# Reordering the beginning of a diffusion trunk: group products between modulation pieces, and two gate pieces moved into the first feed-forward tiles

## What is computed

```python
mod = silu(cond) @ w_mod[0] + b_mod[0]          # six vectors: shift, scale, gate, twice
h   = rms_norm(x, g) * (1 + scale0) + shift0
p   = window means of h minus h, for windows 2, 4, 8, 16, each on its own 256 channels
y   = einsum('blgc,gcd->blgd', p, pool_w) * pool_scale
x   = x + gate0 * rms_norm(y, g)
h   = rms_norm(x, g) * (1 + scale1) + shift1    # input of the feed-forward block
```

## Time and profile before

| | before |
|---|---|
| timed, median of 3 (least, most) | 2003.72 us (2002.95, 2004.3) |
| profiled execution, its own time | 2000.1 us |
| span of the trace | 1998.4 us |
| busy: TensorE, VectorE, ScalarE, GpSimd | 96%, 59%, 46%, 35% |
| mean granted clock of TensorE | 0.984 of full speed |
| transfers | 322.74 MB, mean 162 GB/s |

### The profile page before, as it was taken

One profiled execution on the slowest core, in us unless ns is written; L12 is line 12 of the kernel. 1 busy time (PEld: TensorE's weight loads), 2 busy tenths in 40 slices (PEclk: granted clock), 3 DMA queues, 4 the chain that ended last, 5 costly groups with the idle time before them and its releaser, 6 DMA issues.

```text
span 1998.4 us, 29996 instructions
## 1 busy us (share of the span) xinstructions
PE 1926.6 (96%) x11750; PEld 1708.8 (86%) x11750; DVE 1178.4 (59%) x1793; ACT 928.0 (46%) x1575; POOL 698.9 (35%) x507
## 2 busy tenths in 40 slices
PE   6899999999999989999999999999999979999998
PEld 4789998899996767999987957999987967899986
DVE  3657751666536685777615844777714684777722
ACT  3544442544547645444425325544425444644422
POOL 0233334232345553332343732322342521323342
PEclk8999999999999989999999998999999989999999
DMA  9874456443331147544365655643375513433442
GB/s 398 339 262 127 136 200 231 150 127 119 115 99 38 38 149 307 198 127 125 134 233 183 206 152 211 231 127 120 102 254 179 180 38 116 137 119 125 127 127 74
DMA packets 80139, 322.74 MB, mean 162 GB/s; under 512 B 8976, under 2 KB 17664, under 8 KB 66688
## 3 DMA queue, kind: packets, MB, share of 16 engines
q1 hardware_dynamic: 78496, 318.93, 46.3%
q10 hardware_dynamic: 1504, 1.91, 0.3%
HBM read 315.70 MB, written 5.10 MB: 161 GB/s over the span
## 4 chain that ended last, share of the span: by engine, by line
PE 87%; DVE 4%; DMA 3%; ACT 2%; issue 2%; POOL 1%; SPq 0%; DVEq 0%; POOLq 0%; ACTq 0%
PE pair L1900 18%; PE pair L1902 18%; PE pair L1901 18%; PE pair L1932 8%; PE pair L1933 8%; PE pair L1934 8%; PE pair L1869 2%; PE pair L2053 2%; PE pair L2147 1%; DMA mod_raw<-in_w_mod 1%; DMA raw<-in_ffn_in 1%; PE pair L2278 1%; PE pair L2058 1%; PE pair L2067 1%; PE pair L2252 1%
## 5 line engine op out<-in xcount | busy, mean ns | idle before, releaser
L796 POOL TENSOR_TENSOR w_lo<-raw,w_hi 128x512 fp32r<-128x512 f32 (+1 forms) x375 | 589.8, 1575 | 1052.0 <-ACT w_hi L930 1051.9
L1900 PE MATMUL pair<-h_hi,w_hi 128*128 128x386 f32 (+1 forms) x2008 | 686.6, 342 | 2.1 <-DVE h_lo L1430 2.1
L1902 PE MATMUL pair<-h_hi,w_lo 128*128 128x386 f32 (+1 forms) x2008 | 681.4, 339 | 0.0
L1901 PE MATMUL pair<-h_lo,w_hi 128*128 128x386 f32 (+1 forms) x2008 | 680.7, 339 | 0.0
L1324 DVE TENSOR_TENSOR w_lo<-raw,w_hi 128x512 fp32r<-128x512 f32 x339 | 405.9, 1200 | 330.1 <-ACT w_hi L930 329.8
L930 ACT ACTIVATE w_hi<-raw 128x1024 fp32r<-128x1024 f32 x375 | 392.5, 1051 | 287.9 <-PE pair L1934 227.9
L1900 PEld LDWEIGHTS pair<-h_hi,w_hi 128*128 128x128 f32 (+1 forms) x2008 | 379.0, 189 | 10.9 <-issue 9.6
L1901 PEld LDWEIGHTS pair<-h_lo,w_hi 128*128 128x128 f32 (+1 forms) x2008 | 379.8, 189 | 0.9
L1902 PEld LDWEIGHTS pair<-h_hi,w_lo 128*128 128x128 f32 (+1 forms) x2008 | 379.1, 189 | 0.3
L1489 DVE SCALAR_TENSOR_TENSOR acc<-pair,taps,acc 128x385 f32<-128x385 f32 x176 | 108.8, 618 | 197.4 <-ACT acc L1044 197.3
L1044 ACT ACTIVATE acc<-pair,taps 128x386 f32<-128x386 f32 x176 | 117.3, 666 | 211.7 <-PE pair L1902 211.6
(11 more groups left out here) (304 smaller groups left out, 2109.3 us busy)
## 6 DMA issues: line engine op xcount, KB each, us to landing
raw<-in_ffn_in SPq DMA_DIRECT2D x176, 512.0 KB, 3.5
raw<-in_ffn_out SPq DMA_DIRECT2D x88, 512.0 KB, 3.6
mod_raw<-in_w_mod SPq DMA_DIRECT2D x36, 1024.0 KB, 6.7
mod_base<-in_w_mod SPq DMA_DIRECT2D x31, 1024.0 KB, 7.0
mod_more<-in_w_mod SPq DMA_DIRECT2D x18, 1024.0 KB, 21.5
raw<-in_ssd_conv SPq DMA_DIRECT2D x32, 512.0 KB, 3.5
raw<-in_ssd_z SPq DMA_DIRECT2D x16, 512.0 KB, 3.5
raw<-in_ssd_out SPq DMA_DIRECT2D x16, 512.0 KB, 3.6
```

What stands on the lines that cost most here:

```text
L796: pool.tensor_tensor(w_lo[:, m % SLOTS, 0:w], raw[:, m % SLOTS, 0:w], w_hi[:, m % SLOTS, 0:w].bitcast(F32), ALU.subtract).then_inc(w_low_p ...
L1900: ten.matmul(to, wh, h_hi[:, k, cols], start=k == 0, stop=False, skip_group_check=True)
L1901: ten.matmul(to, wh, h_lo[:, k, cols], start=False, stop=False, skip_group_check=True)
L1902: ins = ten.matmul(to, wl, h_hi[:, k, cols], start=False, stop=k == KD - 1, skip_group_check=True)
```

## The change

Five edits, all in layer 0:

1. The output product of the pool runs per group. A group's product for the blocks starts when its own two channel tiles are ready, and pieces 8 to 11 stand between the groups. The banks of the pool tiles and of vector 1 change so that this is free of conflicts. The two chunks of `pool_w` are rounded one after tile 4 and one after tile 6 of the pool loop instead of both ahead of tile 4, and their low halves stand in VectorE's loop likewise.
2. ScalarE's and VectorE's part of `transition0` is re-ordered; ScalarE's rounding of the first feed-forward chunks goes behind the last sum of squares, and VectorE makes the third `unit_stage` ahead of the second `unit_low`.
3. On TensorE, pieces 12 to 15 go ahead of the first `turn_unit`, 16 and 17 behind the second, 18 and 19 behind the third.
4. Only two of gate1's four pieces run ahead of tile 0; the other two stand behind tiles j = 2 and 3, and the eight pieces of layer 1 behind j = 4 to 11. SyncE's loads are shifted to fit.
5. Gate1 is read by VectorE behind tile 3, and turned behind tile 5 in place of 3.

The hunks are in the order of the file: constants and SyncE, then ScalarE, VectorE and TensorE.

```diff
+GATE1_BEFORE = 2
+GATE1_TURNED_BEHIND = 5
...
-            i = j - INSIDE_FIRST + MOD_PIECES
-            return end_pieces(0)[i] if l == 0 and MOD_PIECES <= i < len(end_pieces(0)) else None
+            i = j - INSIDE_FIRST + GATE1_BEFORE
+            return end_pieces(0)[i] if l == 0 and GATE1_BEFORE <= i < len(end_pieces(0)) else None
...
-                            load_to(s.n0 + INSIDE_FIRST + i + 2)
+                            load_to(s.n0 + INSIDE_FIRST + MOD_PIECES - GATE1_BEFORE + i + 2)
...
             def transition0(n):
                 gate_copy(0)
                 first(0, 0)
+                first(0, 1)
                 gate_copy(1)
-                first(0, 1)
                 second(0, 0)
+                first(0, 2)
                 second(0, 1)
-                first(0, 2)
+                second(0, 2)
                 round_to(n + 2)
-                second(0, 2)
...
-                    if k == POOL_DEPTH:
-                        round_to(2)
+                    if k in (POOL_DEPTH, POOL_DEPTH + 2):
+                        round_to(k // 2 - 1)
...
                 coefficient(0, 1)
                 before_weigh(0, 0)
+                before_weigh(0, 1)
                 weigh(0, 0)
-                before_weigh(0, 1)
                 residual(0, 0)
+                before_weigh(0, 2)
                 weigh(0, 1)
                 residual(0, 1)
                 unit(0, 0)
-                before_weigh(0, 2)
+                weigh(0, 2)
+                residual(0, 2)
                 unit(0, 1)
                 mod_vector(3)
                 coefficient(0, 2)
-                weigh(0, 2)
-                residual(0, 2)
+                unit(0, 2)
                 mod_vector(4)
-                unit(0, 2)
                 unit_stage(0, 0)
                 unit_stage(0, 1)
                 unit_low(0, 0)
+                unit_stage(0, 2)
                 unit_low(0, 1)
-                unit_stage(0, 2)
                 low_to(n + 1)
...
-                mod_vector(phases[1][0])
-                coefficient(0, 3)
...
-                if k == KD:
-                    low_to(2)
+                if k in (POOL_DEPTH + 1, POOL_DEPTH + 3):
+                    low_to(k // 2 - 1)
...
+                v2 = 2 * MOD_PIECES
+                ten.wait_ge(sums_copied, len(WINDOWS))
+                for g in range(2):
+                    mod_piece(v2 + g)
+                    for c in range(3):
+                        ins = product(g, c)
+                ins.then_inc(w_used, 1)
+                mod_piece(v2 + 2)
+                ten.wait_ge(pooled_scaled, KD)
+                for c in range(2):
+                    product(2, c)
+                mod_piece(v2 + 3)
+                for c in range(2):
+                    product(3, c).then_inc(out_done, 1)
+                ten.wait_ge(coef_ready, 2)
+                spread_gate(0)
+                ten.wait_ge(mod_read, 3)
+                product(2, 2)
+                product(3, 2).then_inc(w_used, 1)
+                ten.wait_ge(gate_copied, 1)
+                spread_gate(1)
+                for p in range(3 * MOD_PIECES, 4 * MOD_PIECES):
+                    mod_piece(p)
                 ten.wait_ge(gate_copied, 2)
                 turn_unit(0, 0)
                 ten.wait_ge(pre_ready, 2)
                 turn_unit(0, 1)
+                for p in range(4 * MOD_PIECES, 4 * MOD_PIECES + 2):
+                    mod_piece(p)
                 ten.wait_ge(pre_ready, 3)
                 turn_unit(0, 2)
+                for p in range(4 * MOD_PIECES + 2, START_VECTORS * MOD_PIECES):
+                    mod_piece(p)
                 ten.wait_ge(stage_act, 1)
                 ten.wait_ge(stage_dve, 1)
-                fill(0, 0, MOD_PIECES)
+                fill(0, 0, GATE1_BEFORE)
```

More of the change, by code:

```diff
@@ L342, in pooled_bank @@
         def pooled_bank(k):
-            return bank((6, 7, 0, 1)[k % POOL_DEPTH])
+            return bank((6, 7, 1, 3)[k % POOL_DEPTH])
         def tile_bank(j):
@@ L516, in squares @@
             if t == 0:
-                return 3 + ((0, 2), (1, 3), (4, 5))[c][which]
+                return 3 + ((0, 2), (1, 4), (3, 5))[c][which]
             return 3 + (2 * event(t, c) + which if t < 2 * DEPTH - 1 else 2 * event(t, 0) + c)
@@ L1045, in ffn_in @@
                                    bias=taps[:, l, j, 3:4]).then_inc(acc_ready, 1)
-                    if j == 3:
+                    if j == gate_turned_behind(l):
                         copy_row(2 * l)
@@ L1498, in ffn_in @@
                     low_to(s.n0 + j + 5)
+                    if l == 0 and j == 3:
+                        mod_vector(phases[1][0])
+                        coefficient(0, 3)
                     if l == 0 and j == 7:
@@ L1860, in mod_piece @@
                 ten.wait_ge(mod_loaded[mod_slot[p]], 16 * mod_uses[p])
-                if j == 0 and i == 2:
-                    ten.wait_ge(mod_read, 1)
+                if j == 0 and i in (1, 2):
+                    ten.wait_ge(mod_read, i)
                 if j == 0 and i in (3, 4):
@@ L2325, in pool_mix @@
                 for k in range(KD):
-                    if k in (2, 3):
-                        ten.wait_ge(sums_copied, k - 1)
+                    if k == 2:
+                        ten.wait_ge(sums_copied, 2)
                     if k >= POOL_DEPTH:
@@ L2333, in pool_mix @@
                             mod_piece(p)
-                for p in range(2 * MOD_PIECES, 3 * MOD_PIECES):
-                    mod_piece(p)
-                chunk_ready(0)
-                chunk_ready(1)
-                ten.wait_ge(pooled_lo, KD)
-                for c in range(3):
-                    cols = slice(AT[c], AT[c] + P)
-                    if c == 1:
-                        ten.wait_ge(mod_read, 2)
-                    if c == 2:
-                        ten.wait_ge(mod_read, 3)
-                        ten.wait_ge(sums_copied, len(WINDOWS))
-                    for g in range(4):
-                        to = pair[c][:, g * 256:(g + 1) * 256]
-                        for kk in range(2):
-                            k, at = 2 * g + kk, (2 * (g % 2) + kk) * 256
-                            wh, wl = (v[:, g // 2, at:at + 256] for v in (w_hi, w_lo))
-                            ten.matmul(to, h_hi[:, k, cols], wh, start=kk == 0, stop=False, skip_group_check=True)
-                            ten.matmul(to, h_lo[:, k, cols], wh, start=False, stop=False, skip_group_check=True)
-                            ins = ten.matmul(to, h_hi[:, k, cols], wl, start=False, stop=kk == 1, skip_group_check=True)
-                        if c == 2 and g % 2:
-                            ins.then_inc(w_used, 1)
-                    if c < 2:
-                        ins.then_inc(out_done, 1)
-                        if c == 0:
-                            ten.wait_ge(coef_ready, 2)
-                            ten.wait_ge(pooled_scaled, KD)
-                        else:
-                            ten.wait_ge(gate_copied, 1)
-                        spread_gate(c)
@@ L2364, in pool_mix, with product @@
-                for p in range(3 * MOD_PIECES, 4 * MOD_PIECES - 1):
+                def product(g, c):
+                    chunk_ready(g // 2)
+                    ten.wait_ge(pooled_lo, 2 * g + 2)
+                    cols, to = slice(AT[c], AT[c] + P), pair[c][:, g * 256:(g + 1) * 256]
+                    for kk in range(2):
+                        k, at = 2 * g + kk, (2 * (g % 2) + kk) * 256
+                        wh, wl = (v[:, g // 2, at:at + 256] for v in (w_hi, w_lo))
+                        ten.matmul(to, h_hi[:, k, cols], wh, start=kk == 0, stop=False, skip_group_check=True)
+                        ten.matmul(to, h_lo[:, k, cols], wh, start=False, stop=False, skip_group_check=True)
+                        ins = ten.matmul(to, h_hi[:, k, cols], wl, start=False, stop=kk == 1, skip_group_check=True)
+                    return ins
@@ L2367, in pool_mix @@
                 turn_unit(0, 0)
-                for p in range(4 * MOD_PIECES - 1, START_VECTORS * MOD_PIECES):
-                    mod_piece(p)
                 ten.wait_ge(pre_ready, 2)
                 turn_unit(0, 1)
+                for p in range(4 * MOD_PIECES, 4 * MOD_PIECES + 2):
+                    mod_piece(p)
                 ten.wait_ge(pre_ready, 3)
                 turn_unit(0, 2)
+                for p in range(4 * MOD_PIECES + 2, START_VECTORS * MOD_PIECES):
+                    mod_piece(p)
                 ten.wait_ge(stage_act, 1)
                 ten.wait_ge(stage_dve, 1)
-                fill(0, 0, MOD_PIECES)
+                fill(0, 0, GATE1_BEFORE)
             ten.wait_ge(cond_ready, 1)
```

8 lines of the change are left out of this document (5 added, 3 removed).

## The result

| | before | after |
|---|---|---|
| timed, median (least, most) | 2003.51 us (1996.17, 2006.21), 20 runs | 2008.37 us (2003.62, 2013.62), 20 runs |
| ratio after to before | | 1.0031, 95% interval 1.0023 to 1.0038 |
| profiled execution, its own time | 2000.1 us | 2007.64 us |

The change makes the kernel slower by 0.31%: by the ratio 6.2 us (4.6 to 7.6), by the medians 4.9. The forecast was 5.4 us.

A forecast was written before the change was run, and what follows sets the result against it. The beginning was held by transfers and short chains, then by TensorE's own work from tile 0. Terms 0.9 - 0.8 + 2.4 + 1.1 + 1.8 = 5.4 us on 2003.72 gave 2009.1 us, 8-in-10 range 2003.2 to 2011.5.

The forecast's parts named there:

- both places at half clock: TensorE around the first two turns and at tile 0's start: half clock costs +1.1 and +1.8 us; chance 0.58.
- The step called decisive: TensorE's order puts shift1's last pieces behind the turns, ending at 70.3, so unit_stage waits for them: +0.9 us.
- The rival by which the clock holds: TensorE keeps full clock in one or both places; 2006.2 us if both, chance 0.28 including one.
- The chain that pays: Rival: VectorE's chain ends earlier, tile 0 starts near 75.6; gain at most 3.0 us, 2000.7; chance 0.09.
- First product 39.6, spread 49.6: TensorE's pool products start near 39.6 instead of 45.64; first gate spread follows at 49.6, against 48.53.
- Gate copy, weigh, VectorE's chain 10.6: After the spread: gate copy 2.0 us, weigh done at 53.8, VectorE then runs 10.6 us without waiting, to 64.4.
- `unit_stage` at 71.0, or 72 with the half clock: Start of unit_stage after shift1 is read, against 70.05 before: +0.9 us, later still at half clock.
- exactly the term: Half clock on the two pieces behind the second turn, 0.56 longer each: +1.1 us.
- Tail -0.8: From unit_stage to tile 0, the third unit_stage fills VectorE's idle time, winning 0.8 of 1.8 us.
- Two pieces +2.4: Two gate1 pieces moved from TensorE's wait to between feed-forward tiles cost 1.2 us each: +2.4 us.
- Half clock at tile 0 +1.8: After idling ahead of tile 0, TensorE runs its first about 4.1 us at half clock: +1.8 us.
- Tile 0 at 79.3 to 80.5: Sign expected in the changed profile: first feed-forward tile starts at 79.3 to 80.5, against 79.24 before.

The follow-up runs named there:

- a_turns: Changed kernel with TensorE's pieces 15 to 19 back in the order before the change, all ahead of the second turn; ratio to the kernel before 1.0009.
- b_pieces: Kernel before with only pieces 15 to 19 in the changed order, and shift1 read behind VectorE's third unit; ratio to the kernel before 1.0017.
- b_gate2: Kernel before with only the gate1 part: two pieces ahead of tile 0, two more between tiles, gate row turned later; ratio to the kernel before 1.0012.
- a_gate4: Changed kernel with all four gate1 pieces ahead of tile 0 again; ratio to the kernel before 1.0021.
- a_both: Changed kernel with pieces 15 to 19 ahead of the second turn and four gate1 pieces ahead of tile 0; ratio to the kernel before 1.0001.
- a_warm2: Changed kernel with unread matmuls added on idle TensorE: five before the first turn, four before the second, seven behind the second gate1 piece; ratio to before 1.0021.
- c_tail: c_ahead with VectorE's second unit_low ahead of the third unit_stage again, as before the change; ratio to the kernel before 0.9991.
- b_round: Kernel before with only ScalarE's rounding of the two feed-forward chunks moved behind its last sum of squares; ratio to the kernel before 1.0005.
- c_ahead: Changed kernel with pieces 15 to 19 all ahead of the first turn and four gate1 pieces ahead of tile 0; ratio to the kernel before 0.9989.
- c_early: c_ahead with the products of block 2 with groups 0 and 1 moved behind the first gate spread; ratio to the kernel before 0.9991.
- c_early3: c_early with three gate1 pieces ahead of tile 0 instead of four; ratio to the kernel before 0.9990.
- a_three: a_turns with three gate1 pieces ahead of tile 0 instead of two; ratio to the kernel before 1.0010.

## Why the prediction was right, and where its terms were off

The forecast was 5.4 us with both places at half clock, and the timed difference is 4.9 by the medians and 6.2 by the ratio. The step called decisive was: pieces 18 and 19 behind the third turn hold `unit_stage`. The chain of waits shows it in the trace, and a_turns and b_pieces show what the order of pieces 15 to 19 costs, the one by taking it away (0.22%), the other by doing it alone (0.17%). The second cost, two pieces moved out of a wait, is shown by b_gate2 (0.12%). With a_gate4's 0.10% and a_both's 0.01% for the rest, the parts add up to 0.28 to 0.35%, around the change's 0.31%; each part is known to about 0.1%. The rival by which the clock holds falls with the trace (0.50 through most of 62.8 to 69.6 and 76 to 86.6) and with a_warm2. The chain that pays came out nowhere: tile 0 would have had to start before 76.8.

Term by term, by the trace of after:

- *First product 39.6, spread 49.6.* Measured 39.81 and 50.57. The ten products took 7.8 us where I had 7.2 (0.78 each and not 0.72, the first one of a group being longer behind a piece), the pieces 1.0 each.
- *Gate copy, weigh, VectorE's chain 10.6.* Measured 1.99, 2.19 and 10.5 us. Right.
- *`unit_stage` at 71.0, or 72 with the half clock.* Measured 74.10. Of the 3.1 us over 71.0, 1.0 is the later spread, 1.1 the two pieces at half clock (2.98 for 1.9, exactly the term), 0.9 the second turn at half clock. I had left that turn out, and where I priced one I took 1.40 from the earlier trace rows, a turn that ran only in part at half clock: a whole one takes 1.94.
- *Tail -0.8.* Measured 0.0: 9.18 us from `unit_stage` to tile 0, before 9.19; c_tail confirms it. I saw that the step must wait for GpSimd, and still took half of the idle time as won. It waits 1.27 us, and the low half behind it takes 2.02 where it took 1.57.
- *Two pieces +2.4.* In the trace 97.75 to 98.75 and the longer matmul behind it, 1.2 each, as taken from the earlier trace rows. The other pieces between the tiles and the later gate row were put at nothing; one piece waited 0.5 us for its transfer.
- *Half clock at tile 0 +1.8.* Measured 1.5 (3.4 us at 0.32 for 0.18).
- *Tile 0 at 79.3 to 80.5.* Measured 83.28, outside what was named as a sign. The path was right and the terms on it were too small.

By the two traces the loss is larger than forecast: 8.6 us up to the marker, and 7.5 between the two profiled executions as a whole. The terms ahead of tile 0 were too small by 2.8 us (+1.2 said, +4.0 found); behind it 4.2 were said and 4.6 found, of which 0.5 is the wait for a transfer. That the timed 4.9 to 6.2 lies so near the 5.4 is therefore luck in part: the sum was too small for the pair of executions that were traced, and that pair lies further apart than the timed runs do. The execution traced before was 3.4 us faster than its median, the one after only 0.7.

The clock in the products does not explain that gap. Both traces have it full there. In the three other traces with the old order the four products ahead of the first spread took 1.3 to 2.4 us longer; in five of the eight traces with the ten products of the new order ahead of it these took 1.3 to 1.5 us longer. By these means the old order loses some 0.6 us more than the new one, an estimate from few traces. The new product order was never run alone, so what it gives back, and where the rest of the gap lies, stays open.

From the marker to the end it takes 1593.4 us (a_turns) to 1600.1 (b_round), whatever the edit. Why, stays open too, and it is why a single trace can't stand for the timed difference.

## What to carry to other kernels

A piece of filler work belongs ahead of the work that waits for its data, in the engine's idle time, not behind it: behind the last step of a chain it becomes the last step. Before such a piece is moved, ask who reads its result and where that reader then stands. And where an engine idles ahead of a long dense stretch, the work that fills that wait costs nothing and can keep TensorE's clock; moving it into the dense stretch costs its length and often, on top, the slow start. c_ahead is the version to take; its gain over the kernel before is 0.4 to 4.2 us by its interval, and c_early, c_early3 and c_tail can't be told from it.

## What the runs showed of the hardware

The half clock came back where TensorE had waited between short bursts, but not after every such wait and not always in the same place: the same four products ahead of the first spread ran at full clock in one trace and wholly or in part at half clock in three. At tile 0, idle times of 4.74, 5.71, 4.83 and 5.77 us (after, a_turns, a_three, b_gate2) led to half clock, and one of 2.33 to 2.51 us to full clock (a_gate4, b_pieces, a_warm2); but a_both, with 2.71, had half clock, b_round, with 4.05, kept the full clock for its first matmuls only, and c_tail entered half clock in its last gate piece without any longer wait than c_ahead, which kept its clock. With four gate pieces ahead, tile 0 began at full clock in four traces (before, a_gate4, b_pieces, c_ahead) and wholly or partly at half clock in four (a_both, b_round, c_early, c_tail); with two or three pieces and nothing else in the wait it began at half clock in all five. The Trainium skill (TensorE: Matmul & The Clock Gate, "HAM oscillation — how this bites in real kernels") describes the pattern, and its half of the cold time as the loss is close: 0.44 here.

VectorE and GpSimd hold each other up when both read two blocks at once, and which one pays depends on who is there first. With GpSimd idle a low half of 512 columns takes VectorE 0.64 us (1.28 for two, in c_tail at 77.38), and an undisturbed weight half takes GpSimd 1.25 us (2.50 for two, c_ahead). In c_tail VectorE's low half of 1024 columns (74.01 to 75.57) starts during GpSimd's first weight half and took 1.56 us; GpSimd's second one, begun at 74.45, then took 2.25 us. In c_ahead VectorE comes later, at 75.20, when the second one is already under way (74.87 to 76.15): GpSimd is not slowed, and VectorE takes 2.02. The Trainium skill (SBUF — State Buffer, "Who interferes with whom") calls this an exclusive lock, under which the later one stands still, and the rows agree: in both traces the lengths are near what they are alone plus the wait for the other one's instruction to end.

The gate row turned between tiles waited for VectorE's coefficient in some executions with three or four gate pieces ahead. TensorE's waits between 85 and 410 us in c_tail, one of several rows:

```profile
PE pair L1884 <- DVE coef L1353: 1.8, 1, 1.8
```

In c_early it is 2.0 us, in a_gate4 1.5, in a_both, a_three and c_early3 0.4; in c_ahead there is none, and none in the kernels with two gate pieces ahead. Why it comes in one execution and not in another stays open; turning that row a tile later was not tried.
